# Second block's attention: value products once per head with 512 query columns, and two instead of four buffers for rounded weights in its background

## Chip, cores and metric

The kernel runs on one core of a Trainium2 chip. The metric is the device time of one execution in microseconds (us), the median of the timed runs. Engines: PE is the matmul engine (TensorE), PEld its weight load, DVE is VectorE, ACT is ScalarE, POOL is GpSimd, and SP issues DMAs.

## The reference, cut to what matters

Two transformer-like blocks run one after the other on 512 tokens with 1024 channels, in float32. The change lies in the second block's attention. It has 8 heads of two 64-wide halves and 128-wide values:

```python
def one_block(q_blk):                                   # 128 queries
    s = einsum('bqhcd,bkhcd->bhcqk', q_blk, k) * scale  # c: the two halves
    p = softmax(s, axis=-1)
    p_diff = p[:, :, 0] - lam * p[:, :, 1]
    return einsum('bhqk,bkhd->bqhd', p_diff, v)
```

Around it: `h = rms_norm(x)`; `q, k, v, lru_x, lru_g, gates = split(h @ w_in)`; q and k are normalised and rotated; the attention's result is normalised per head and multiplied by `w_attn_o`; `lru_x` goes through a convolution over time and a gated linear recurrence, `lru_g` through a gelu. Both branches are gated, added and multiplied by `w_out`; a mixture of experts follows.

## The kernel before, in words

Activations lie with channels on the 128 partitions and the 512 tokens along the free dimension. The large projections run in a split form (`product3`, line 1045): the weight is rounded to fp32r (the upper part, made by ACT, helper `weights2_upper`, line 1453, which records line 1428), the rest is the lower part (made by DVE, recorded as line 2053, or by POOL, line 2877), and each 128-channel product is 24 matmuls of 512 columns (line 1057). `JOBS_2` is the written list of these products: 16 for q and k, 8 for v, then `lx` 0 to 7, `lg` 0 to 7 and the rest. Upper parts go into four buffers `up2` (two in the tile `o`, two in `zp`) up to job 31, two others after that. ACT rounds a weight four jobs ahead (two ahead from `lg` on).

Products write to `acc`, a ring of four accumulators in PSUM. `accumulator` (line 774) takes the next one and makes PE wait until the reader of the product four before has finished. Each engine's program is in order; nothing but semaphores joins them.

The attention runs in `STEPS2` = 35 steps over 32 items (8 heads, four tiles of 128 queries each; item s is head s // 4, tile s % 4). In step s PE does: scores of item s (two halves, 512 keys, K = 64, line 1133); in steps 4, 8, 13, 17, 21, 26, 30 and 34 one background product `lx` (`background2_at`); the four transposes of item s - 2 (line 1141); the values of item s - 3 (four fp32 matmuls, 128 query columns, line 1150). An fp32 matmul is two records in the trace. DVE does in step s: the maximum of item s (lines 2450, 2451), then `weigh` of item s - 1 (lines 2439 to 2443), which turns two exponentials into the weighed difference. ACT does: two exponentials of item s (line 1752), then, where there is a background product, its copy into `lru_x` (line 1756) and the rounding of a later weight, then the copy of the transposed weights into one of four buffers `probsT2` (line 1765), and the copy of the values' 128 columns into `q2` (line 1768). `probsT2` lies in the tile `upad` (`padf`). POOL takes the low part of a weight (`lx` 4 to 7) in front of the convolution of `lx` c = 0 to 3, then the convolution itself (lines 2903 to 2908); c = 4 to 7 have the convolution alone.

Before the loop stand the v product (line 1121), ACT's copies of it (line 1736) with two roundings per group of it, DVE's low parts of jobs 20 to 27 (the v weights' last four and `lx` 0 to 3) and DVE's sums for lambda (lines 2424 to 2433). After it PE has the `lg` products, DVE a chain of small operations named decay.

Of the kernel before, what the change touches and what calls it, by code (L numbers as in the profile page):

```python
# [22 lines left out]
P = 128  # L23
# [53 lines left out]
S = SEQ  # L77
# [122 lines left out]
def program(nc, a, out, known=None, debug=None):  # L200
    n = Counts(known)
    mark, at, now = n.mark, n.at, n.now
    with ExitStack() as ctx:
# [124 lines left out]
        padf = upad[:, :, :].rearrange("p c t -> p (c t)")  # L328
        probsT2 = [padf[:, i * S:(i + 1) * S].rearrange("p (j q) -> p j q", j=QT) for i in range(4)]
        cos2, sin2 = trig[:, 0, 0:S], trig[:, 1, 0:S]  # L330
# [222 lines left out]
        job_no2 = {x[0]: i for i, x in enumerate(JOBS_2)}  # L553
        EARLY2 = job_no2["lg", 0]
        up2 = [x[:, :, :].rearrange("p c t -> p (c t)")[:, i * D:(i + 1) * D].rearrange("p (k m) -> p k m", k=DC)
# [4 lines left out]
        def weight2_up(i):  # L560

            return up2[i % 4] if i < EARLY2 else up2_late[i % 2]

# [8 lines left out]

        LOW_BY_POOL = [job_no2["lx", c] for c in range(4, DC)]

# [190 lines left out]
        def _(pe):  # L765
# [378 lines left out]

            def values2(s):
                hd, i = items2[s]
                pe.wait_ge(act_evacuated, at(act_evacuated, ("t2", s)))
                dst = accumulator(("o2", s), act_evacuated)
                for j in range(QT):
                    ins = nc.tensor.matmul(dst[:, 0, 0:P], v2[:, j, hd * P:(hd + 1) * P], probsT2[s % 4][:, j, :],  # L1150
                                           start=(j == 0), stop=(j == QT - 1))
                done(ins, ("o2", s))

            for s in range(STEPS2):
                if s < len(items2):
                    scores2(s)
                for c in background2_at(s):
                    product3(("lx", c), act_evacuated, h2_up, h2_low)
                if 2 <= s < len(items2) + 2:
                    turn2(s - 2)  # L1160
                if s >= 3:
                    values2(s - 3)
            for c in range(DC + LAG):
# [236 lines left out]
        def _(act):  # L1400
# [53 lines left out]
            def weights2_upper(i):  # L1454

                if i < len(JOBS_2):
                    label, name, j = JOBS_2[i]
                    slot = place2[name]
                    act.wait_ge(w2_loaded[slot], at(w2_loaded[slot], name))
                    if i < 4:  # L1460
                        act.wait_ge(psum_filled, at(psum_filled, ("ym" if i < 2 else "out", DC - 1)))
                    elif i == EARLY2:
                        act.wait_ge(dve_made, at(dve_made, ("qkr", 2 * DC - 1)))
                    elif i == EARLY2 + 1:
                        act.wait_ge(psum_filled, at(psum_filled, ("t2", len(items2) - 1)))
                    else:
                        act.wait_ge(psum_filled, at(psum_filled, job_done(i - (4 if i < EARLY2 else 2))))
                    upper(weight2_up(i), columns2(name, j), ("wup",) + label)
# [263 lines left out]
            for g in range(4):  # L1732
# [5 lines left out]
                for j in range(2):  # L1738
                    weights2_upper(2 * DC + 4 + 2 * g + j)

            act.wait_ge(dve_made, at(dve_made, "lam_sums"))
            made(nc.scalar.activation(small[:, 10:12], small[:, 8:10], ACT.Exp), "lam_exp")
            for s in range(STEPS2):
# [11 lines left out]
                for c in background2_at(s):  # L1755
                    evacuated(nc.scalar.activation(lru_x[:, c, 1:1 + S], result2(("lx", c)), ACT.Copy), ("lx", c))
                    if job_no2["lx", c] + 4 < EARLY2:
                        weights2_upper(job_no2["lx", c] + 4)
                if s == STEPS2 - 4:
                    weights2_upper(EARLY2)  # L1760
                if 2 <= s < len(items2) + 2:
                    src = result2(("t2", s - 2)).rearrange("p (j q) -> p j q", j=QT)
                    if s >= 6:
                        act.wait_ge(psum_filled, at(psum_filled, ("o2", s - 6)))
                    evacuated(nc.scalar.activation(probsT2[(s - 2) % 4], src, ACT.Copy), ("t2", s - 2))
                if s >= 3:
                    hd, i = items2[s - 3]
                    evacuated(nc.scalar.activation(q2[:, hd, i * P:(i + 1) * P], result2(("o2", s - 3))[:, 0:P],
                                                   ACT.Copy), ("o2", s - 3))
            weights2_upper(EARLY2 + 1)  # L1770
            act.wait_ge(dve_made, at(dve_made, "neg_abs"))
            made(nc.scalar.activation(decay[:, 1, :], decay[:, 1, :], ACT.Exp), "lam_e")
            def output_squares(c):
                if c >= 2:
                    act.wait_ge(psum_filled, at(psum_filled, ("oss", c - 2)))
                act.wait_ge(act_evacuated, at(act_evacuated, ("o2", len(items2) - 1)))
                made(nc.scalar.activation(tmp[c % 2], q2[:, c, :], ACT.Square), ("sqo", c))
# [218 lines left out]
        def _(dve):  # L1996
# [411 lines left out]
            for c in range(2 * DC + 1):  # L2408
# [8 lines left out]
                if c < 2 * DC:  # L2417
                    weights2_lower(c + 4)
            for i in range(2 * DC + 4, 2 * DC + 12):
                weights2_lower(i)  # L2420
# [101 lines left out]
            for m in range(DC):  # L2522
                if m == 0:
                    dve.wait_ge(act_evacuated, at(act_evacuated, ("o2", len(items2) - 1)))
                if m:
# [244 lines left out]
        def _(pool):  # L2770
# [120 lines left out]
            for c in range(DC):  # L2891
                if c < 4:
                    weights2_lower(job_no2["lx", 4 + c])
                if c == 0:
# [80 lines left out]
```

## Time and profile before

| | us |
|---|---|
| median of 3 runs | 2028.38 (2026.44 to 2030.29) |
| profiled execution | 2031.49 |
| its span | 2029.70 |

| engine | busy us | share of the span |
|---|---|---|
| PE | 1865.5 | 92% |
| PEld | 1550.7 | 76% |
| DVE | 1190.3 | 59% |
| ACT | 891.8 | 44% |
| POOL | 355.7 | 18% |

Busy times are of one execution; the span is the time from its first to its last instruction, the profiled time has 1.79 us around it. The granted clock is PE's, as a share of 2.4 GHz. The attention of the second block runs from 1150.6 to about 1308 us of the span.

### The profile page before, as it was taken

To read this page: it belongs to the slowest core of one execution; us is meant where nothing else is said; L and a number is where in the kernel's file an instruction comes from. 1 tells how busy PE (TensorE), PEld (TensorE's weight loads), DVE (VectorE), ACT (ScalarE), POOL (GpSimd) and SP (SyncE) were. 2 spreads that over 40 slices of the span, in tenths; PEclk is the share of its full clock that TensorE was granted. 3 is DMA by queue.
4 is the path that set the end of the run, shared out by engine and by line. 5 is a ranking of instruction groups with operands and counts; after the bars stand their busy time and mean duration, and the time that the engine had idled before them with its cause. 6 is when DMAs were issued, how large, how long until landed. Compare 5 with 4: busy or idle time off the path is not lost.

```text
span 2029.7 us, 26888 instructions
## 1 busy us (share of the span) xinstructions
PE 1865.5 (92%) x10912; PEld 1550.7 (76%) x10912; DVE 1190.3 (59%) x1628; ACT 891.8 (44%) x1425; POOL 355.7 (18%) x239
## 2 busy tenths in 40 slices
PE   6999999999999999999898888989999997999993
PEld 5988787989997788988676765665568876777772
DVE  5565443445375543543787467567664337788786
ACT  4435433324435443322332355336643235777672
POOL 3332221002333221002311055500000001000001
PEclk9999999999999999999898999999999988999997
DMA  5212102223212202223121200121333237999994
GB/s 170 68 63 68 42 22 83 63 65 123 81 38 88 63 22 84 63 74 128 42 83 42 83 21 22 42 84 42 104 135 107 101 112 275 373 386 379 377 375 166
DMA packets 155949, 241.61 MB, mean 119 GB/s; under 512 B 9313, under 2 KB 100738, under 8 KB 155826
## 3 DMA queue, kind: packets, MB, share of 16 engines
q1 hardware_dynamic: 148450, 213.07, 31.0%
q0 software_dynamic: 4464, 16.25, 2.1%
q10 hardware_dynamic: 2912, 10.55, 1.3%
q8 instruction: 88, 1.44, 0.3%
q14 instruction: 35, 0.29, 0.0%
HBM read 223.61 MB, written 16.25 MB: 118 GB/s over the span
## 4 chain that ended last, share of the span: by engine, by line
PE 77%; DVE 16%; ACT 3%; issue 2%; DMA 1%; POOL 1%; SPq 0%; ACTq 0%; POOLq 0%; DVEq 0%
PE acc L825 27%; PE acc L1057 16%; PE acc L1269 9%; PE acc L1042 4%; PE acc L924 4%; PE acc L988 3%; PE acc L1121 2%; DVE ring_split L2637 2%; PE acc L965 2%; DVE ring_split L2053 1%; DVE v L2388 1%; PE acc L1179 1%; DVE rt L2450 1%; PE acc L842 1%; PE acc L976 1%
## 5 line engine op out<-in xcount | busy, mean ns | idle before, releaser
L825 PE MATMUL acc<-h_split,ring_split 128*128 128x264 f32 x1088 | 310.0, 285 | 0.0
L825 PEld LDWEIGHTS acc<-h_split,ring_split 128*128 128x128 f32 x1088 | 206.2, 190 | 0.0
L1057 PE MATMUL acc<-h_split,ring_split 128*128 128x512 f32 x368 | 146.1, 397 | 0.0
L825 PE MATMUL acc<-h_split,v_split 128*128 128x264 f32 x384 | 111.6, 291 | 19.0 <-DVE ring_split L2053 19.0
L825 PE MATMUL acc<-ring_split,v_split 128*128 128x264 f32 x384 | 109.9, 286 | 0.0
L2388 DVE RECIPROCAL v<-v 128x512 f32<-128x512 f32 x26 | 87.1, 3351 | 27.9 <-ACT v L1706 27.9
L825 PE MATMUL acc<-h_split,krope_split 128*128 128x264 f32 x320 | 94.8, 296 | 4.1 <-ACT latent L1607 2.6
L825 PE MATMUL acc<-ring_split,krope_split 128*128 128x264 f32 x320 | 91.5, 286 | 0.0
L825 PEld LDWEIGHTS acc<-h_split,v_split 128*128 128x128 f32 x384 | 73.4, 191 | 22.0 <-issue 22.0
L2053 DVE TENSOR_TENSOR ring_split<-ring,o_split 128x1024 fp32r<-128x1024 f32 (+1 forms) x32 | 47.0, 1473 | 73.6 <-ACT o_split L1428 73.6
L2921 POOL DMA_INDIRECT latent<-h_rows,rows_of x16 | 18.4, 1148 | 396.8 <-PE acc L1255 229.5
L2791 POOL TENSOR_TENSOR latent<-latent 128x528 f32<-128x528 f32 x18 | 28.5, 1583 | 338.4 <-ACT latent L1423 338.0
L2053 DVE TENSOR_TENSOR ring_split<-ring,v_split 128x1024 fp32r<-128x1024 f32 (+1 forms) x56 | 59.8, 1071 | 44.0 <-ACT v_split L1428 44.0
L1269 PE MATMUL acc<-qk_split,krope_split 128*128 128x512 f32 x240 | 75.8, 397 | 8.5 <-DVE ring_split L2637 6.2
L1057 PEld LDWEIGHTS acc<-h_split,ring_split 128*128 128x128 f32 x368 | 70.2, 191 | 16.3
L2805 POOL TENSOR_TENSOR ring_split<-ring,krope_split 128x1024 fp32r<-128x1024 f32 x20 | 48.3, 2414 | 168.9 <-ACT krope_split L1428 168.9
L988 PE MATMUL acc<-latent,v 128*64 128x128 f32 (+2 forms) x464 | 74.1, 284 | 0.9 <-ACT latent L1627 0.8
L1428 ACT ACTIVATE v_split<-ring 128x1024 fp32r<-128x1024 f32 (+2 forms) x58 | 54.8, 949 | 43.3 <-PE acc L825 41.8
L825 PEld LDWEIGHTS acc<-ring_split,v_split 128*128 128x128 f32 x384 | 73.5, 191 | 0.0
L825 PE MATMUL acc<-work_split,v_split 128*128 128x264 f32 x256 | 72.9, 285 | 0.0
L825 PE MATMUL acc<-upad_split,ring_split 128*128 128x264 f32 x256 | 72.7, 284 | 0.0
L2637 DVE TENSOR_TENSOR ring_split<-ring,qk_split 128x2048 fp32r<-128x2048 f32 x24 | 54.1, 2295 | 27.2 <-ACT qk_split L1924 27.2
(557 smaller groups left out, 5766.8 us busy)
## 6 DMA issues: line engine op xcount, KB each, us to landing
ring<-in_w_in SPq DMA_DIRECT2D x64, 1024.0 KB, 5.3
ring<-in_w_expert_gate SPq DMA_DIRECT2D x13, 2048.0 KB, 10.0
ring<-in_w_expert_up SPq DMA_DIRECT2D x12, 2048.0 KB, 11.1
ring<-in_w_expert_down SPq DMA_DIRECT2D x11, 2048.0 KB, 11.5
ring<-in_w_out SPq DMA_DIRECT2D x12, 1024.0 KB, 5.2
hres<-in_w_expert_down SPq DMA_DIRECT2D x5, 2048.0 KB, 10.9
hres<-in_w_expert_up SPq DMA_DIRECT2D x4, 2048.0 KB, 10.9
y_rows<-gate ACTq DMA_DIRECT2D x16, 512.0 KB, 7.2
```

Of the source, the lines that this page charges most:

```text
L825: ins = nc.tensor.matmul(dst[0:rows_, half, 0:HALF], w[:, k, :], x[:, c], start=(k == 0 and i == 0), stop=(k == last and i == 2), skip_gro ...
L924: ins = nc.tensor.matmul(dst[0:nt, half, 0:width], x, w[:, c], start=(k == 0 and part == 0), stop=(k == count - 1 and part == 2), skip_gro ...
L965: ins = nc.tensor.matmul(dst[0:nt, c0:c1], qT[0:QK, hd, t0:t0 + nt], kT[0:QK, hd, c0:c1], start=True, stop=True)
L988: ins = nc.tensor.matmul(dst[r:r + VD, 0, 0:nt], v[0:nk, j, hd * VD:(hd + 1) * VD], probsT[s % 2][0:nk, j, 0:nt], start=(j == 0), stop=(j ...
L1042: ins = nc.tensor.matmul(dst[:, 0, :], w, rhs(k), start=(k == 0), stop=(k == len(lhs) - 1))
L1057: ins = nc.tensor.matmul(dst[:, 0, :], w[:, k, :], x, start=(k == 0 and i == 0), stop=(k == DC - 1 and i == 2), skip_group_check=True)
L1269: ins = nc.tensor.matmul(dst, x, w, start=start and i == 0, stop=stop and i == 2, skip_group_check=True)
L1428: nc.scalar.activation(dst, src, ACT.Copy).then_inc(act_made, 1)
L2053: made(nc.vector.tensor_tensor(dst, src, up.bitcast(F32), ALU.subtract), label)
L2388: chain(nc.vector.reciprocal(tmp[tile], tmp[tile]))
L2637: nc.vector.tensor_tensor(granule_half(i, half, "low"), granule_half(i, half, "raw"), granule_half(i, half, "up").bitcast(F32), ALU.subtra ...
L2805: nc.gpsimd.tensor_tensor(dst, src, up.bitcast(F32), ALU.subtract).then_inc(pool_made, 1)
```

## The change

1. `values2` is called once per head, behind the transposes of its last tile (steps 6, 10, ... 34): four matmuls with 512 query columns in place of sixteen with 128. ACT copies the result once per head, 512 columns wide.
2. `probsT2` has two buffers for a whole head each, one in `upad`, one in `zp`. ACT waits once per head for a free one.
3. As `zp` is taken, the upper parts of `lx` use the two buffers in `o` alone, and are made two products ahead. `lx` 2 and 3 are no longer rounded before the loop but in it.
4. The low parts of `lx` 2 and 3 go from DVE (before the loop) to POOL (in front of convolutions 0 and 1), so POOL makes six of them.

```diff
-        probsT2 = [padf[:, i * S:(i + 1) * S].rearrange("p (j q) -> p j q", j=QT) for i in range(4)]
+        probsT2 = [x[:, 0:QT * S].rearrange("p (j q) -> p j q", j=QT) for x in (padf, flat_of(zp))]
...
-        EARLY2 = job_no2["lg", 0]
+        EARLY2, LX2 = job_no2["lg", 0], job_no2["lx", 0]
...
-            return up2[i % 4] if i < EARLY2 else up2_late[i % 2]
+            return up2[i % 4] if i < LX2 else up2[i % 2] if i < EARLY2 else up2_late[i % 2]
...
-        LOW_BY_POOL = [job_no2["lx", c] for c in range(4, DC)]
+        LOW_BY_POOL = [job_no2["lx", c] for c in range(2, DC)]
...
-            def values2(s):
-                hd, i = items2[s]
-                pe.wait_ge(act_evacuated, at(act_evacuated, ("t2", s)))
-                dst = accumulator(("o2", s), act_evacuated)
+            def values2(hd):
+                pe.wait_ge(act_evacuated, at(act_evacuated, ("t2", QT * hd + QT - 1)))
+                dst = accumulator(("o2", hd), act_evacuated)
                 for j in range(QT):
-                    ins = nc.tensor.matmul(dst[:, 0, 0:P], v2[:, j, hd * P:(hd + 1) * P], probsT2[s % 4][:, j, :],
+                    ins = nc.tensor.matmul(dst[:, 0, :], v2[:, j, hd * P:(hd + 1) * P], probsT2[hd % 2][:, j, :],
                                            start=(j == 0), stop=(j == QT - 1))
...
-                if s >= 3:
-                    values2(s - 3)
+                if s >= 3 and items2[s - 3][1] == QT - 1:
+                    values2(items2[s - 3][0])
...
-                        act.wait_ge(psum_filled, at(psum_filled, job_done(i - (4 if i < EARLY2 else 2))))
+                        act.wait_ge(psum_filled, at(psum_filled, job_done(i - (4 if i < LX2 + 2 else 2))))
...
                 for j in range(2):
-                    weights2_upper(2 * DC + 4 + 2 * g + j)
+                    if 2 * DC + 4 + 2 * g + j < LX2 + 2:
+                        weights2_upper(2 * DC + 4 + 2 * g + j)
...
-                    if job_no2["lx", c] + 4 < EARLY2:
-                        weights2_upper(job_no2["lx", c] + 4)
+                    if job_no2["lx", c] + 2 < EARLY2:
+                        weights2_upper(job_no2["lx", c] + 2)
...
-                    if s >= 6:
-                        act.wait_ge(psum_filled, at(psum_filled, ("o2", s - 6)))
-                    evacuated(nc.scalar.activation(probsT2[(s - 2) % 4], src, ACT.Copy), ("t2", s - 2))
-                if s >= 3:
-                    hd, i = items2[s - 3]
-                    evacuated(nc.scalar.activation(q2[:, hd, i * P:(i + 1) * P], result2(("o2", s - 3))[:, 0:P],
-                                                   ACT.Copy), ("o2", s - 3))
+                    hd, i = items2[s - 2]
+                    if hd >= 2 and i == 0:
+                        act.wait_ge(psum_filled, at(psum_filled, ("o2", hd - 2)))
+                    evacuated(nc.scalar.activation(probsT2[hd % 2][:, :, i * P:(i + 1) * P], src, ACT.Copy), ("t2", s - 2))
+                if s >= 3 and items2[s - 3][1] == QT - 1:
+                    hd = items2[s - 3][0]
+                    evacuated(nc.scalar.activation(q2[:, hd, :], result2(("o2", hd)), ACT.Copy), ("o2", hd))
...
-            for i in range(2 * DC + 4, 2 * DC + 12):
+            for i in range(2 * DC + 4, LX2 + 2):
                 weights2_lower(i)
...
             for c in range(DC):
-                if c < 4:
-                    weights2_lower(job_no2["lx", 4 + c])
+                if c + 2 < DC:
+                    weights2_lower(job_no2["lx", c + 2])
```

## Rows read from the trace of the kernel before

**Rows 1.** The page's busy times: us, share of the span, instructions.
```profile
PE 1865.5 (92%) x10912; PEld 1550.7 (76%) x10912; DVE 1190.3 (59%) x1628; ACT 891.8 (44%) x1425; POOL 355.7 (18%) x239
```
**Rows 2.** A stretch: its us, busy PE, PEld, DVE, ACT, POOL; granted clock, DMA.
```profile
1210.00:1230.00 20.00, 17.56 (x97) 12.43 (x96) 12.65 (x24) 9.96 (x26) 11.68 (x8) 1.00 0.00 1
```
**Rows 3.** Waits in the loop: who for whom, us in total, times, longest.
```profile
POOL v L2903 <- ACT latent L1756: 32.8, 4, 11.4
...
DVE rt L2450 <- PE acc L1133: 36.8, 8, 5.3
```
**Rows 4.** Chain of waits, one period: start us, length, engine, tile, line.
```profile
1218.92 1.14 DVE rt L2450
...
1222.45 1.15 DVE rt L2450
...
1225.38 5.83 PE acc L1057 x24
...
1233.64 1.24 DVE rt L2450
```
**Rows 5.** PE's timeline there: start us, length, line, form [idle before, what ended it].
```profile
1218.97 0.66 PE L1141 MATMUL acc<-const,krope 128*128 128x128 f32 x4 [1.25 <-DVE krope L2443]
...
1222.51 0.66 PE L1141 MATMUL acc<-const,v 128*128 128x128 f32 x4 [0.93 <-DVE v L2443]
1223.00 1.06 PE L1150 MATMUL acc<-upad,work 128*128 128x128 f32 x8
1223.99 1.13 PE L1133 MATMUL acc<-qk 64*128 64x512 f32 x4
1225.38 0.50 PE L1057 MATMUL acc<-h_split,zp_split 128*128 128x512 f32 x1 [0.26 <-ACT krope L1752]
```
**Rows 6.** PE's timeline later: fp32 products of 512 columns.
```profile
1358.87 1.88 PE L1042 MATMUL acc<-v,ones 128*128 128x512 f32 x4
```
**Rows 7.** Timeline of ACT and DVE at the loop's start.
```profile
1150.68 0.60 ACT L1736 ACTIVATE work<-acc 128x512 f32<-128x512 f32 x1 [5.08 <-PE acc L1121]
...
1151.17 1.99 ACT L1428 ACTIVATE zp_split<-ring 128x1024 fp32r<-128x1024 f32 x2
...
1152.25 2.36 DVE L2053 TENSOR_TENSOR ring_split<-ring,zp_split 128x1024 fp32r<-128x1024 f32 x2 [8.99 <-ACT zp_split L1428]
...
1153.18 1.28 ACT L1742 ACT_TABLE_LOAD   x1
...
1155.42 0.20 ACT L1742 ACTIVATE small<-small 128x2 f32<-128x2 f32 x1 [0.96 <-DVE small L2425]
...
1156.08 1.20 DVE L2450 TENSOR_REDUCE rt<-acc 128x2 f32<-128x1024 f32 x1
```
**Rows 8.** PE's timeline at the loop's end and before lg 2.
```profile
1295.54 1.12 PE L1141 MATMUL acc<-const,gate 128*128 128x128 f32 x4 [2.62 <-DVE gate L2443]
...
1301.54 0.52 PE L1057 MATMUL acc<-ring_split,zp_split 128*128 128x512 f32 x1
...
1321.23 0.47 PE L1057 MATMUL acc<-h_split,trig_split 128*128 128x512 f32 x1 [2.05 <-DVE ring_split L2053]
```
**Rows 9.** PE's timeline behind idle times; by stretch: us, PE busy, granted clock, DMA.
```profile
350.69 0.56 PE L825 MATMUL acc<-h_split,v_split 128*128 128x264 f32 x1 [2.79 <-DVE ring_split L2053]
...
808.49 0.36 PE L825 MATMUL acc<-h_split,v_split 128*128 128x264 f32 x1 [2.79 <-DVE ring_split L2053]
...
1256.13 0.66 PE L1141 MATMUL acc<-const,gate 128*128 128x128 f32 x4 [1.57 <-DVE gate L2443]
...
1321.00:1327.00 6.00, 5.77 (x18) 0.72 0.49 144
...
1509.58 0.51 PE L1057 MATMUL acc<-latent_split,krope_split 128*128 128x512 f32 x1 [1.95 <-DVE o_split L2053]
...
1664.98 6.34 PE L1224 MATMUL acc<-const,h 128*128 128x128 f32 x32
...
1670.00:1671.00 1.00, 1.00 (x9) 0.78 0.01 4
```

More of the change, by code:

```diff
@@ L1143, in turn2 @@
                 done(ins, ("t2", s))
-            def values2(s):
-                hd, i = items2[s]
-                pe.wait_ge(act_evacuated, at(act_evacuated, ("t2", s)))
-                dst = accumulator(("o2", s), act_evacuated)
+            def values2(hd):
+                pe.wait_ge(act_evacuated, at(act_evacuated, ("t2", QT * hd + QT - 1)))
+                dst = accumulator(("o2", hd), act_evacuated)
                 for j in range(QT):
-                    ins = nc.tensor.matmul(dst[:, 0, 0:P], v2[:, j, hd * P:(hd + 1) * P], probsT2[s % 4][:, j, :],
+                    ins = nc.tensor.matmul(dst[:, 0, :], v2[:, j, hd * P:(hd + 1) * P], probsT2[hd % 2][:, j, :],
                                            start=(j == 0), stop=(j == QT - 1))
-                done(ins, ("o2", s))
+                done(ins, ("o2", hd))
             for s in range(STEPS2):
@@ L1775, in output_squares @@
                     act.wait_ge(psum_filled, at(psum_filled, ("oss", c - 2)))
-                act.wait_ge(act_evacuated, at(act_evacuated, ("o2", len(items2) - 1)))
+                act.wait_ge(act_evacuated, at(act_evacuated, ("o2", HEADS - 1)))
                 made(nc.scalar.activation(tmp[c % 2], q2[:, c, :], ACT.Square), ("sqo", c))
@@ L2523, in _ @@
                 if m == 0:
-                    dve.wait_ge(act_evacuated, at(act_evacuated, ("o2", len(items2) - 1)))
+                    dve.wait_ge(act_evacuated, at(act_evacuated, ("o2", HEADS - 1)))
                 if m:
```

## Prediction

> **What bounds the kernel now.** I read the busy times of the page first: the matmul engine works 92% of the span [rows 1], so at most places the kernel goes at its pace. The changed stage is the second block's attention, from 1150.6 to about 1308 us. The busy times of a stretch in its middle show no engine full: PE 17.6, DVE 12.7, ACT 10.0 and POOL 11.7 us of 20, with the clock at 1.00, 2.4 GHz [rows 2]. So waits decide. The table of waits has one large entry on the way: DVE's score maximum waited 36.8 us for the scores, in 8 pieces of up to 5.3 us [rows 3]. The chain of waits over one period says why [rows 4]: steps at DVE's pace (maxima start at 1218.92 and 1222.45, 3.53 apart), then the background product lx (1225.38, 5.83 long), behind it transposes, values and scores, and the next maximum only at 1233.64. From 1222.45 to 1233.64 are 11.2 us for two DVE steps; DVE starves. Seven products lie so inside the loop.
>
> **1. The values.** Before, each of 32 steps has 8 records with 128 columns; they start at 1223.00 and the scores behind them at 1223.99, so they take 0.99 [rows 5]. Per head that is 4 x 0.99 = 3.96. Afterwards a head has 8 records with 512 columns. No fp32 product of this stage has that shape; the ones products of the same engine do, four of them in 1.88 us, each lasting 0.59 [rows 6]: (1.88 - 0.59) / 3 = 0.43 apart, so 8 x 0.43 = 3.44. PE's own work shrinks by about 0.5 us a head, 4 us in all, if all of it were on the path. But it comes as one lump behind every fourth step.
>
> **2. The ring of four accumulators.** Every product takes the next of 4, and waits until the one taken four before is read. Before, in front of lx lie the scores of its step, the values, the transposes and the scores of the step before: lx waits for the exponential of the step before. It shows in [rows 5]: scores start at 1223.99, and lx at 1225.38 after idle time that ACT's exponential ended. Without values in each step that place holds older transposes, read long ago. So nothing but PE's own order holds lx.
>
> **3. One period at full clock.** Transposes start at 1222.51 [rows 5], values would follow at 1223.00. Now scores stand there and hold PE 1.13 less a drain of some 0.07, up to 1224.06; lx then takes its 5.83 less 0.16, as its first matmul doesn't start cold, up to 1229.73; transposes 0.43 (0.66 less the drain), 1230.16; scores to the maximum 1.17, 1231.33, instead of 1233.64. (The three differences are estimates from the starts and durations of rows 4 and 5.) This saves 2.31 where no values come. Products fall in steps 4, 8, 13, 17, 21, 26, 30, 34, and whole heads are multiplied in steps 6, 10, 14, 18, 22, 26, 30, 34, both from the floor rule and from the four tiles a head. So:
> - five products without values in their step: 5 x -2.31 = -11.55;
> - steps 26 and 30 hold both, 3.44 more between product and maximum: 2 x (3.44 - 2.31) = +2.26;
> - steps 6 and 10: transposes 0.49, values 3.44, scores 1.17 make 5.10 us, and 0.06 before it, where DVE needs 3.53 [rows 4]: 2 x 1.63 = +3.26;
> - steps 14, 18, 22 the same, and the values wait for a copy that ACT makes behind the copy of lx and the rounding of a weight; some 0.4 more: 3 x 2.03 = +6.1.
>
> The sum is +0.1: the time won by the earlier product is given back by the lumps. The lower bound lets the five products gain 2.9 each, were DVE and the drains 0.6 quicker there, -3; the upper has the wait of 0.4 in all lumps and 0.5 more at each product, +4.
>
> **4. The start.** ACT rounds two weights (1151.17, 1.99 for both) and DVE takes two low parts (1152.25, 2.36) right behind the v product; then DVE sums lambda, and ACT's exponential is at 1155.42, the first maximum at 1156.08 [rows 7]. These are lx 2 and 3, which move into the loop. DVE's sums then are made during the v product, ACT loads its table (1.28) where the roundings stood, behind the copy that ends at 1151.28, so the exponential falls at 1152.57: -2.85, on the path since scores 0 follow the v product at once. Bounds: 0 (another wait) and -3.5.
>
> **5. The end.** Before, the last product starts at about 1301 (its second matmul at 1301.54), behind transposes and values at half clock: those at 1295.54 last 1.12 [rows 8] instead of 0.66 [rows 5]. Without those two values it starts with the last transposes' end, near 1298.9: -2.1; but it then runs at half clock for some 2 us more, +1.05. Behind it 3.44 instead of 0.99: +2.45; ACT's copy is 512 wide (0.60 instead of 0.28): +0.32. All that follows hangs on this copy: ACT's rounding for lg 1, DVE's low part, the decay work, and PE again at 1321.23 after 2.05 idle [rows 8]. Sum +1.7; bounds 0 and +3.
>
> **6. The background's weights.** Rounding lx 2 to 7 (1.05 each) moves from four products ahead to two. ACT does it behind the copy of each product, POOL takes the low part, now for six products instead of four. A low part and the seven pieces of a convolution are the 8 instructions and 11.68 us of POOL in [rows 2], and a period has 18 us, later perhaps 16; POOL waited 32.8 us in all for lx [rows 3]. The product that reads it comes two periods later. So I count 0; without that cover each product would wait for ACT's rounding (1.0) and POOL's low part, which I put at 2 (DVE takes 1.2, rows 7): 3 each. No DMA is moved: slots of raw weights come free by the same products.
>
> Without the clock the sum is 0.1 - 2.85 + 1.7 = -1.1 us.
>
> **7. The clock.** PE's idle before the transposes in a DVE-paced step is 1.25 and 0.93 [rows 5]; once 1.57, and the clock stayed at 2.4 GHz [rows 9]. Taking 0.99 of values away makes these 2.2, 1.9 and 2.5. The same trace went to 1.2 GHz around idles of 1.95 and 2.05, and 2.62 [rows 8, 9]. There are about 13 such gaps in the new loop, two in each early period, three in the late ones. From 1321 to 1327 the granted clock is 0.72 in the mean [rows 9]: with only the levels 1.0 and 0.5, that is 0.28 x 6 / 0.5 = 3.4 us at half, which loses 1.7 us of PE work if PE is full. In plain steps DVE hides that: transposes and scores doubled (0.86 + 2.12) are 3.0 of 3.5. Before lx or a lump it is paid. I take three falls at 1.2: +3.6. Bounds: none, 0; eight at 1.7, +13.6. That a gap of such length does not always cost is in [rows 9]: of two idles of 2.79 us before the same kind of matmul one was followed by a slow one (0.56), the other by one at its normal 0.36. I take the lower side since half of each fall is hidden in plain steps.
>
> The Trainium skill, "TensorE: Matmul & The Clock Gate", Part 4, holds that transposes don't count as activity for the clock, which would leave the plain steps with scores alone and make most of the 13 gaps fall (about 8, +13.6 instead of +3.6). In this trace 32 transposes run alone from 1664.98 for 6.3 us, and the clock granted from 1670 to 1671, inside them, is 0.78 in the mean [rows 9]: with two levels only, it rose among transposes. So I don't take the rule, though it feeds rival B.
>
> **The sum.** -1.1 + 3.6 = +2.5 us. The profiled execution took 2031.49 (span 2029.70), so it would be 2034.0; the median of the timed runs is 2028.38, 3.1 less, so I say 2030.9. A change within 0.2% (4.06 us) can't be told from none here.
>
> **Rivals.**
> - A: the clock never falls inside the loop. For: gaps of 1.57 passed. Against: 1.95 and 2.05 fell. With sum -1.1 it gives 2027.3; with the low ends of 3 (-3) and 5 (0) it is -5.9, 2022.5. Chance 0.30, about 0.18 of it faster.
> - B (slower): half clock in most gaps, PE's activity being too thin without the values. For: idle grows over the two lengths that fell. Against: gaps are parted by 6 to 9 us of full work. Six to eight falls at 1.7: +9 to +12.5, 2037.5 to 2041. It decides from three falls at 1.7 (-1.1 + 5.1 = +4.0). Chance 0.27.
> - C: lx does not start earlier, as ACT holds an accumulator for another reason. Then only the 0.99 is saved by five products, 5 x 1.32 = 6.6 more: +9, 2037.5. The ring's order speaks against it. Chance 0.05.
> - D: POOL's low parts are late from lx 2 on: 6 x 3 = +18. POOL's slack is against it. 0.03.
>
> The forecast's own case (one to four falls, 2027 to 2033) has 0.35. Faster: 0.18 from A and 0.02 from the forecast's low end, 0.20. Same: 0.12 of A and 0.30 of the forecast, 0.42. Slower: 0.03 of the forecast, B, C and D, 0.38. The range 2023.5 to 2038.5 takes A nearly whole and B's nearer half.
>
> **What would show it.** Step 2: lx starts with no idle after its scores. Step 3: the maximum comes 8.9 us after the one two steps before at lx, instead of 11.2, and 12.3 in steps 26 and 30. Step 4: first maximum 2.8 us nearer to the v product's end. Step 5: 3.4 us from the last lx to its copy. Step 7: granted clock under 1.00 between 1170 and 1290, where it was 1.00. If the clock stays at 1.00 and the loop is still not shorter by 1, my lumps are wrong; if the loop is over 8 us shorter, the price of the lumps is.

## The result, and the profile after

The changed kernel takes 2042.56 us (median of 5 runs, 2042.07 to 2048.88), the kernel before 2029.05 beside it (2026.44 to 2032.23): a ratio of 1.0072, 95% interval 1.0053 to 1.009 (here and below the times are medians; a ratio is worked out from the single executions and can differ a little from the quotient of the medians). It is slower by 13.5 us, and above the range of the prediction. The profiled execution took 2043.05 (span 2041.2) against 2031.49 before. From the first scores of the loop to the decay work behind the last product are 159.9 us before and 173.4 after, so the loss lies in the changed loop. Of the ten executions of the first experiment two were slow (4755.98 and 10062.9 us); they count in its median and not in its ratio.

The busy times of the page, as in [rows 1]:

```profile
PE 1874.4 (92%) x10720; PEld 1535.2 (75%) x10720; DVE 1199.1 (59%) x1626; ACT 889.2 (44%) x1401; POOL 360.1 (18%) x241
```

PE has 192 instructions fewer (32 x 8 values became 8 x 8) and is yet busy 9 us longer. DVE has two instructions fewer and is busy 9 us longer. Work of the same kind has become slower on both.

By stretch (us, busy PE, PEld, DVE, ACT, POOL; granted clock, DMA), the first as in [rows 2]:

```profile
1210.00:1230.00 20.00, 17.03 (x64) 9.06 (x63) 15.44 (x25) 10.08 (x24) 11.99 (x8) 0.91 0.01 1
...
1224.00:1230.00 6.00, 4.03 (x12) 2.07 (x13) 5.80 (x9) 3.07 (x8) 4.46 (x3) 0.72 0.00 0
```

The clock is 0.91 where it was 1.00. The six us of the second row hold 0.28 x 6 / 0.5 = 3.4 us at 1.2 GHz, behind an idle time of PE. From 1170 to 1290 the clock falls six times (near 1177.5, 1198, 1225.5, 1246, 1266.5 and 1287) and is 0.92 in the mean; before it fell there not once and was 1.00. Outside these bounds both kernels have a fall at the loop's start (near 1157 and 1158) and one at its end (1307.5 and 1295). "Falls" below are those from 1170 to 1290.

The waits, as in [rows 3]:

```profile
DVE rt L2450 <- PE acc L1133: 40.3, 13, 6.6
...
POOL v L2903 <- ACT latent L1756: 16.9, 2, 9.7
```

DVE starves as much as before (40.3 us for 36.8), in 13 pieces instead of 8. What the edit was to cure is only cut up differently: a long wait at each product became a shorter one there and another at the values.

The chain of waits over one period, as in [rows 4] (start us, length, engine, tile, line):

```profile
1229.10 5.79 PE acc L1057 x24
1234.89 0.44 PE acc L1141 x4
1235.33 1.06 PE acc L1133 x4
1236.38 0.59 PE acc L1141 x4
...
1237.01 3.70 PE acc L1149 x8
1240.71 1.08 PE acc L1133 x4
...
1241.81 1.24 DVE rt L2450
...
1244.66 1.64 DVE gate L2443
...
1246.35 1.11 PE acc L1141 x4
1247.46 2.01 PE acc L1133 x4
1249.47 0.75 PE acc L1057 x2
```

From product to product are 20.4 us; before, 18.4 (products at 1206.96, 1225.38, 1243.79). The first 12.7 are as forecast: the product, a light step, the values of a head, scores. Then comes one whole step of DVE, 4.5 us from 1241.81 to 1246.35 and not 3.53. And PE, idle during it, comes back at half clock: transposes 1.11 instead of 0.66, scores 2.01 instead of 1.06.

PE's timeline shows the idle time, as in [rows 5] (in brackets the idle before and what ended it):

```profile
1197.51 5.29 PE L1149 MATMUL acc<-zp,work 128*128 128x512 f32 x8
...
1216.63 3.70 PE L1149 MATMUL acc<-upad,work 128*128 128x512 f32 x8
...
1225.97 1.12 PE L1141 MATMUL acc<-const,v 128*128 128x128 f32 x4 [2.94 <-DVE v L2443]
1227.02 2.08 PE L1133 MATMUL acc<-qk 64*128 64x512 f32 x4
```

The idle is 2.94, where before it was 0.93 to 1.57 [rows 5, 9]. The values of a head take 3.70 with a full clock and 5.29 where the clock has just fallen.

And DVE's and POOL's timelines show why a step of DVE takes 4.5:

```profile
1216.05 1.23 DVE L2450 TENSOR_REDUCE rt<-acc 128x2 f32<-128x1024 f32 x1 [3.17 <-PE acc L1133]
1217.31 1.22 DVE L2451 TENSOR_SCALAR rt<-rt 128x2 f32<-128x2 f32 x1
...
1224.29 1.63 DVE L2443 SCALAR_TENSOR_TENSOR v<-v,rt 128x512 f32<-128x512 f32 x1
```
```profile
1216.16 2.34 POOL L2877 TENSOR_TENSOR ring_split<-ring,o_split 128x1024 fp32r<-128x1024 f32 x1 [11.50 <-ACT o_split L1427]
...
1224.06 1.31 POOL L2907 TENSOR_TENSOR v<-v 128x512 f32<-128x512 f32 x1
```

L2451 scales two numbers per partition. It takes 0.17 where it is alone and here 1.22: it ends at 1218.53, when POOL's low part L2877 ends (1218.50). L2443 takes 0.75 alone and 1.63 across POOL's L2907, a piece of the convolution. In the critical step from 1221.43 to 1225.92 the convolution adds 0.25 + 0.30 + 0.88 = 1.43 us to three operations. Over the loop DVE's six operations sum to 115.3 us, before to 104.8. In a run in which POOL has next to nothing to do in the loop (below) they sum to 96.1, so they are stretched by 19.2 us, before by 8.7.

The kernel before has the same operations in another phase:

```profile
1215.22 1.23 DVE L2450 TENSOR_REDUCE rt<-acc 128x2 f32<-128x1024 f32 x1 [5.27 <-PE acc L1133]
1216.48 0.33 DVE L2451 TENSOR_SCALAR rt<-rt 128x2 f32<-128x2 f32 x1
```
```profile
1214.44 2.35 POOL L2877 TENSOR_TENSOR ring_split<-ring,zp_split 128x1024 fp32r<-128x1024 f32 x1 [9.22 <-ACT zp_split L1428]
```

There POOL's low part, which starts when ACT has rounded the weight behind its copy of the product, lay 2.0 us under DVE's wait and under the maximum. Behind the product came values (0.99) ahead of the scores. Without them the maximum comes 1 us earlier against POOL, and L2451 runs into the low part.

The Trainium skill, "SBUF — State Buffer", section "Who interferes with whom", says that DVE and GpSimd share a port pair that is an exclusive lock, that beside a DVE operation in a two-port mode, which a tensor_scalar can enter, the later of the two "fully blocks", and that a tensor_reduce never contends on this chip. The trace agrees in both: L2451, a tensor_scalar, ends with POOL's operation, and all 32 maxima take 1.20 to 1.23 us. Whether L2451 runs in such a mode no run shows.

### The profile page after: what moved, and what is told of

The parts are those of the page before. It is cut to its first block, busy times and chain, and to the rows that moved or that the text cites. A ratio compares the mean times of both kernels' runs of the same rounds, so it can differ in the third digit from the quotient of the medians.

```text
span 2041.2 us, 26434 instructions
## 1 busy us (share of the span) xinstructions
PE 1874.4 (92%) x10720; PEld 1535.2 (75%) x10720; DVE 1199.1 (59%) x1626; ACT 889.2 (44%) x1401; POOL 360.1 (18%) x241
## 4 chain that ended last, share of the span: by engine, by line
PE 79%; DVE 14%; ACT 2%; issue 2%; DMA 1%; POOL 1%; SPq 0%; ACTq 0%; POOLq 0%; DVEq 0%
PE acc L825 27%; PE acc L1057 16%; PE acc L1268 9%; PE acc L1042 4%; PE acc L924 4%; PE acc L988 3%; PE acc L1121 2%; DVE ring_split L2637 2%; PE acc L965 2%; PE acc L1149 2%; DVE v L2388 1%; DVE ring_split L2053 1%; PE acc L1178 1%; PE acc L842 1%; PE acc L1133 1%
## 5 line engine op out<-in xcount | busy, mean ns | idle before, releaser
L2921 POOL DMA_INDIRECT latent<-h_rows,rows_of x16 | 18.1, 1130 | 397.6 <-PE acc L1254 231.2
```

## The experiments

Theory P (POOL): the new phase puts POOL's operations across DVE's critical steps. Theory C (clock): PE's thinner work lets the clock fall. Theory L (lumps): a head's values behind every fourth step make PE and DVE take turns. All runs were timed beside the kernel before. "Stretch" below is the sum of DVE's six operations in the loop less 96.1. "The loop" in us is from its first scores to the decay work, in the profiled execution.

**Values per tile again, with the new buffers of weights.**

```diff
-            def values2(hd):
+            def values2(s):
...
-                if s >= 3 and items2[s - 3][1] == QT - 1:
-                    values2(items2[s - 3][0])
+                if s >= 3:
+                    values2(s - 3)
```

> The changed kernel with the values again per tile (16 products of 128 columns a head, an accumulator for each step), but with its two big buffers, its rounding of lx two products ahead and its six low parts on POOL. Theory (the lump of 512 columns makes the loss): the loop goes at the old pace, clock 1.00 from 1170 to 1290, and the start keeps its gain, so 2026 to 2027 us, 2 to 3 under the kernel before. Rival (the background's weights cost, by POOL's or ACT's order): 2035 or more, and DVE operations in the loop stretched as in the changed kernel.

Measured: 2028.55, ratio 0.9994 [0.9984, 1.0004], 1.5 above the expected range. No fall, stretch 9.1. So the two buffers, the later rounding and two more low parts on POOL cost nothing by themselves; all of the loss comes with the values. The loop is 3.2 us shorter in its profile (156.7), but the median doesn't show it. In this profile the loop starts 2.7 us later than before (1153.31 against 1150.57); over all runs its start varies from 1148.2 to 1153.3, so one profile can't say where the 3.2 go.

**Products of nothing in the gaps,** three of 512 columns, unread, ahead of the wait for the weights of seven steps.

```diff
+                dst = accumulator(("t2", s), act_evacuated)
+                if s + 2 in (6, 10, 16, 20, 24, 28, 32):
+                    for _ in range(3):
+                        nc.tensor.matmul(dst[:, 1, :], ident, v2[:, 0, 0:S], start=True, stop=True)
+                pe.wait_ge(dve_made, at(dve_made, ("p2", s)))
-                dst = accumulator(("t2", s), act_evacuated)
```

> The changed kernel with three fp32 products of 512 columns (2.6 us of PE), whose result nobody reads, ahead of the wait for the weights in steps 6, 10, 16, 20, 24, 28 and 32, where PE idles some 3 us. Theory (half clock): the granted clock stays at 1.00 there and 6 to 7 falls of 1.5 us go: 2032 to 2034. Rival (starving DVE behind the lump and DVE operations stretched by POOL make the loss): 2040 to 2043, clock or not.

Measured: 2039.94, ratio 1.0058 [1.0041, 1.0075], the rival's figure; two falls instead of six, clock 0.96. The idle before the transposes is 0.17 to 0.27 in five of the seven places. But only 2.6 us come back, and stretch goes up from 19.2 to 21.5: with PE sooner back, DVE's steps meet POOL differently. Filling the gaps is no cure, and the clock alone isn't the loss.

**Values of 8 columns instead of 512,** in PE's products and in ACT's copy (leaves out most of the attention's result).

```diff
-                    ins = nc.tensor.matmul(dst[:, 0, :], v2[...], probsT2[hd % 2][:, j, :],
+                    ins = nc.tensor.matmul(dst[:, 0, 0:8], v2[...], probsT2[hd % 2][:, j, 0:8],
```

> The changed kernel with 8 instead of 512 query columns in the values (the attention's result is left out but for 8 columns): no lump, PE even thinner. If the lump is what starves DVE: the loop shrinks by 15 to 25 us, 2018 to 2028, even if the clock falls. If thin work on PE is the cause (my rival B as I put it): the clock falls at least as often and the time stays at 2035 or more.

Measured: 2025.36, ratio 0.9983 [0.9973, 0.9993]. PE has 8 x 2.6 = 21 us less to do, and 17.2 come back. So the lumps are nearly wholly on the path, as the prediction had them. Yet with next to no values at all the kernel is only 3.2 us faster than the kernel before beside it (2028.52); the clock still falls six times and stretch is 14.7. What hurts stays when the values are gone.

**The convolution of POOL on 8 columns** (leaves out most of it), in the changed kernel and in the kernel before.

```diff
-                y, z = tmp[2], tmp[3]
+                y, z = tmp[2][:, 0:8], tmp[3][:, 0:8]
...
-                    x, w = lru_x[:, c, j:j + S], vec2[...]
+                    x, w = lru_x[:, c, j:j + 8], vec2[...]
```

> The changed kernel with POOL's convolution on 8 instead of 512 columns (the rest of it is left out). Theory (DVE's operations are stretched by POOL's): DVE's two-column scaling never lasts over 0.2 us, its weighing never over 0.8; DVE's busy time in the loop falls by 10 us or more, and the time by 5 to 9, 2034 to 2037. If contention is off the path: under 2 us.

> The kernel before with POOL's convolution on 8 instead of 512 columns (the rest is left out). Theory (the change moved DVE's operations under POOL's, and before they fell beside them): DVE's stretch in the loop goes from 10 us to about 1, and the time falls only by 2 to 4, 2025 to 2027, against 18 that the same edit took from the changed kernel. Rival (the convolution costs both the same): 2009 to 2013, and then POOL is no cause of the difference.

Measured: changed 2024.85, ratio 0.9977 [0.9967, 0.9986]; before 2017.82, ratio 0.9943 [0.9925, 0.9961]. The convolution costs the changed kernel 17.7 us and the kernel before 11.2. That is 6.5 of the 13.5. I had expected 5 to 9 and 2 to 4: part of it lies outside the loop, which is shorter by 15.7 (157.7) and 7.3 (152.7). Falls in the changed loop go from six to one with it, so POOL's share in them is large: it makes DVE's steps, and so PE's gaps, longer. Stretch is 5.3, all of it L2451 behind a low part, five times 1.05; in the kernel before it is 0.6.

**POOL's low part behind the convolution.**

```diff
-                if c + 2 < DC:
-                    weights2_lower(job_no2["lx", c + 2])
...
+                if c + 2 < DC:
+                    weights2_lower(job_no2["lx", c + 2])
```

> The changed kernel with POOL's low part of a weight behind the convolution of its turn instead of ahead of it. Theory (where POOL's operations fall against DVE's sets the loss): the five stretches of 1.05 by the low part go or move, all other pieces shift by 3.4 us against DVE; DVE's stretch changes by several us and the time with it, 2035 to 2041, though no work is taken away. Rival (lumps and clock alone): 2042 to 2043.

Measured: 2042.11, ratio 1.0073 [1.0054, 1.0093], stretch 20.8, four falls. This is the rival's figure, not mine: another order of the same operations moves the collisions (stretch 20.8 against 19.2) and wins nothing.

**Values per tile in the unused half of the transposes' accumulator,** so that they take no place in the ring of four; with the old buffers, and with the new ones.

```diff
-                dst = accumulator(("o2", s), act_evacuated)
+                if s + 1 < len(items2):
...
+                    jobs[-1] = (("o2", s), act_evacuated, n.layer)
+                    dst = acc[:, (len(jobs) - 1) % ACCS, 1:2, :]
...
```

> The kernel before, with the values of a tile written into the unused half of the transposes' accumulator of the same step, so that they take no place in the ring of four; 128 columns as before. Theory (the gain of the change is in the ring, where lx no longer waits for the exponential, not in the wide values): lx starts 1.3 us earlier, 7 times, 2019 to 2021, clock 1.00 from 1170 to 1290. Rival (POOL's collisions with DVE eat it, as lx and DVE shift against each other): 2027 or more.

> The same with the change's two large buffers and its rounding two ahead, values per tile: adds the start's 2.8 us, 2016 to 2019. Rival as before: 2026 or more; or the start's gain doesn't reach the end, as in the run with values per tile, then equal to the former.

Measured: 2025.45, ratio 0.9982 [0.9973, 0.9992], and 2024.38, ratio 0.9982 [0.9969, 0.9996]. Both are faster than before, by 3 to 4 us; I had expected 8 to 13. The start's gain of the second doesn't show in its median. The chain of the first shows that the product follows its scores at once (1206.37 + 1.06 = 1207.43):

```profile
1206.37 1.06 PE acc L1133 x4
1207.43 5.75 PE acc L1057 x24
```

The next product is at 1225.51, 18.1 us on, before 18.4. The ring's wait was thus real and worth 0.3 a period, as [rows 5] shows it (0.26 idle); the rest of my 2.31 was the values themselves, which come back as lumps.

**One product of 8 columns per tile, in the kernel before** (leaves out nearly all of the attention's result; ACT copies 8 columns too). This thins PE's work and has neither lumps nor new buffers.

```diff
-                for j in range(QT):
-                    ins = nc.tensor.matmul(dst[:, 0, 0:P], v2[...], probsT2[s % 4][:, j, :],
+                ins = nc.tensor.matmul(dst[:, 0, 0:8], v2[...], probsT2[s % 4][:, 0, 0:8],
```

> The kernel before with one product of 8 query columns instead of four of 128 per tile (the attention's result is left out but for a part); an accumulator per step as before. It takes some 0.7 us from between the transposes and the scores in each step, without lumps and without a change of the ring. Theory (taking this time away moves DVE's scaling under POOL's low part, and thins PE): stretches of up to 1 us appear beside the low parts, DVE's stretch grows from 10 us by 3 or more, PE's idle pieces pass 2 us, and the loop gains less than half of the 0.7 x 7 = 5 it saves behind the products: 2026 to 2029. Rival (no such effect): 2022 to 2024.

Measured: 2031.08, ratio 1.0012 [1.0002, 1.0021]. Taking some 0.7 us of work out of each of 32 steps makes the kernel 2.6 us slower, where I had expected it as fast or 2 us faster. Its loop is 163.4 against 159.9. The granted clock from 1170 to 1290 is 0.83 (PE busy 96.97 us; the columns are those of the stretches above):

```profile
1170.00:1290.00 120.00, 96.97 (x401) 60.63 (x400) 86.00 (x156) 59.37 (x166) 65.17 (x46) 0.83 0.09 27
```

Five falls, and stretch 14.0 instead of 8.7. Both marks of the changed kernel are there without a single lump.

**The same, with the convolution on 8 columns.**

> The kernel before with the thin values (one product of 8 columns per tile) and POOL's convolution on 8 columns; the rest of both is left out. To be set against the kernel before with the short convolution alone (2017.8). If the clock loses time by itself: falls in the loop in PE's gaps of 2 us, and 2018 to 2022 though PE has 0.7 us less per step. If POOL's stretch was the cause of the thin values' loss: no or one fall in the loop, and 2011 to 2014.

Measured: 2018.14, ratio 0.9948 [0.9932, 0.9965], two falls, stretch 3.7. Against 2017.82 with full values the difference is 0.3, for 15 us less work on PE in the stretch from 1170 to 1290 (busy 94.95 against 109.88). By what I had written beforehand this is the outcome in which the clock loses time by itself: two of the five falls stay without POOL's convolution. In the profiles the thin values lengthen the loop by 3.4 with the convolution and shorten it by 2.2 without (150.5 against 152.7). So the larger part of the penalty for thin work comes by way of POOL and a smaller one doesn't, within the noise of some 2 us.

**One us of nothing put back where the values were,** four unread products of 128 columns behind the transposes of the steps with a product of the background.

```diff
+                if len(background2_at(s + 2)) and s + 2 < len(items2):
+                    for _ in range(4):
+                        nc.tensor.matmul(dst[:, 1, 0:P], ident, v2[:, 0, 0:P], start=True, stop=True)
```

> The changed kernel with four fp32 products of 128 columns (1.0 us of PE, read by nobody) behind the transposes of the six steps 4, 8, 13, 17, 21 and 26 (and 30), where they stand between a background product and DVE's next maximum. More work on the path, but DVE's maximum comes 1.0 later against POOL's low part, as before the change. Theory: the five stretches of 1.05 by the low part go and the time does not grow, 2039 to 2043. Rival (no part of the loss is this meeting): the stretches don't matter and the time grows by 6 to 7 us, 2048 to 2050.

Measured: 2042.28, ratio 1.0059 [1.0042, 1.0076]. The phase is put right (the second fence is POOL's):

```profile
1218.05 1.23 DVE L2453 TENSOR_REDUCE rt<-acc 128x2 f32<-128x1024 f32 x1 [4.05 <-PE acc L1133]
1219.31 0.33 DVE L2454 TENSOR_SCALAR rt<-rt 128x2 f32<-128x2 f32 x1
```
```profile
1217.27 2.35 POOL L2880 TENSOR_TENSOR ring_split<-ring,o_split 128x1024 fp32r<-128x1024 f32 x1 [11.49 <-ACT o_split L1430]
```

The scaling is back from 1.22 to 0.33, stretch by the low part is 0.8 instead of 5.3, and all of it is 11.6 instead of 19.2. The time is the changed kernel's, though PE has 7 us more to do. So stretch is no measure of the loss by itself: it counts where it lies on the path. But this also says that the 1.05 at the scaling is mostly not on the path by itself: it lies beside a lump of values, behind which DVE has 0.81 idle (1221.43 in the step above). That the low part costs by holding the convolution back, into the critical step, fits the next run but not the one with the low part behind the convolution, which holds it back no more and took 2042.11; it is not shown.

**Low parts of the background by DVE,** in the steps in which it starves.

```diff
-        LOW_BY_POOL = [job_no2["lx", c] for c in range(2, DC)]
+        LOW_BY_POOL = []
...
+                for c in background2_at(s):
+                    if 2 <= c + 1 < DC:
+                        weights2_lower(job_no2["lx", c + 1])
```

> The changed kernel with the low parts of lx 2 to 7 made by DVE (1.2 us each), behind the weighing in the steps with a background product, where DVE starves, instead of POOL (2.35 each). Theory: the five stretches of 1.05 go, POOL's work is 14 us less and ends earlier, DVE's own 1.2 is partly hidden: 2036 to 2040. Rival (clock and lumps alone): 2042 or more, as DVE has more to do.

Measured: 2038.21, ratio 1.0039 [1.0025, 1.0053], four falls. 4.4 us come back although DVE has six operations more.

**And the convolution on 8 columns besides:** next to nothing of POOL in the loop (leaves out most of the convolution).

> The changed kernel with the low parts by DVE and POOL's convolution on 8 columns (the rest left out): POOL has next to nothing in the loop. Theory: five stretches of 1.05 less than in the changed kernel with the short convolution (2024.9), so 2018 to 2021, and one fall or none in the loop; against 2017.8 (the kernel before with the short convolution) that is the price of the lumps less the gain at the start, 1 to 3. Rival: 2024 or more, the lumps cost 7 by themselves.

Measured: 2019.46, ratio 0.9954 [0.9937, 0.9971], stretch 0 by its definition. No fall until 1287.5, behind an idle time of 2.57 at the loop's end, where the kernel before has one of 2.62 [rows 8]. This is the run on which the case rests most. PE's timeline, two periods:

```profile
1215.16 0.66 PE L1141 MATMUL acc<-const,v 128*128 128x128 f32 x4 [1.51 <-DVE v L2443]
...
1232.70 0.66 PE L1141 MATMUL acc<-const,gate 128*128 128x128 f32 x4 [1.51 <-DVE gate L2443]
```

and DVE's step ahead of the first:

```profile
1212.06 1.23 DVE L2450 TENSOR_REDUCE rt<-acc 128x2 f32<-128x1024 f32 x1 [2.33 <-PE acc L1133]
1213.32 0.17 DVE L2451 TENSOR_SCALAR rt<-rt 128x2 f32<-128x2 f32 x1
...
1214.36 0.75 DVE L2443 SCALAR_TENSOR_TENSOR v<-v,rt 128x512 f32<-128x512 f32 x1
```

DVE's critical step is 3.06 (to 1215.12) instead of 4.49: shorter by the 1.43 read above. PE's gap shrinks by the same, from 2.94 to 1.51; the clock holds; and a period is 17.5 us, not 20.4. The kernel before with the short convolution has 17.4 (transposes at 1199.47, 1216.87, 1234.25).

**The best version:** values per tile in the other half, the new buffers, low parts by DVE.

> Values per tile in the other half of the transposes' accumulator, the change's two large buffers and rounding two ahead, and the low parts of lx by DVE in the 5 us in which it starves: no lump, POOL relieved. Theory: 1 to 3 us under the run with other half and buffers, 2021 to 2024, the best of all. Rival: DVE's work is on the path, 2028 or more.

Measured: 2024.87, ratio 0.997 [0.9956, 0.9985]. It beats both kernels, by 0.2 to 0.3% the one before and by some 0.9% the changed one, and lies 0.9 above the range that I expected. From the version without DVE's low parts it can't be told.

## Why the prediction was wrong

**Steps 1 and 2, the values and the ring: right.** A head's values take 3.45 to 3.70 where the clock is full (3.44 forecast), and the product follows its scores without idle.

**Step 3, one period: right in what PE does, wrong in what DVE does.** Behind a product the next maximum but one comes after 10.6 us (1225.84 to 1236.43), 1.4 of it half clock, so 9.2 for the 8.9 forecast. With a lump it is 5.38 more (to 1241.81), forecast 5.10. But the period leaves one full DVE step on the path, and for it I put 3.53 from [rows 4], a duration that had the collisions of the old phase in it. Here it is 4.5: +1.0 a period. With POOL's convolution short, and in the changed kernel the low parts gone from POOL too, the two run at 17.5 and 17.4 a period, so the "given back by the lumps" of step 3 holds within 0.2.

**Step 4, the start: right.** From ACT's copy of the v product to the first maximum were 5.4 us [rows 7] and are 2.57; the 2.85 forecast came as 2.83. ACT's and then DVE's timeline:

```profile
1151.35 0.60 ACT L1735 ACTIVATE work<-acc 128x512 f32<-128x512 f32 x1 [5.08 <-PE acc L1121]
1151.97 1.28 ACT L1742 ACT_TABLE_LOAD   x1
1153.26 0.20 ACT L1742 ACTIVATE small<-small 128x2 f32<-128x2 f32 x1
```
```profile
1153.92 1.20 DVE L2450 TENSOR_REDUCE rt<-acc 128x2 f32<-128x1024 f32 x1
```

**Step 5, the end: right in kind, and helped by luck.** The timeline of PE and the chain of waits, for [rows 8]:

```profile
1311.23 0.63 PE L1057 MATMUL acc<-ring_split,o_split 128*128 128x512 f32 x1
```
```profile
1311.00 7.20 PE acc L1057 x24
1318.21 3.45 PE acc L1149 x8
...
1333.72 2.33 PE acc L1057 x9
```

From the second matmul of the last product to PE's start on lg 2 are 22.5 us, before 19.7: +2.8. Of this product, lump and copy the forecast had 3.8 (1.05 + 2.45 + 0.32). Up to the decay work it is 4.4 more (13.4 against 9.0), the product's half clock being 1.4; but the decay work is 1.6 shorter (9.1 against 10.7), since fewer of its small operations meet POOL, and that I had not foreseen. Whether the 2.1 ahead of it came can't be read, as the loop in front runs otherwise.

**Step 6, the background's weights on POOL: "So I count 0" is the step that failed.** I asked whether POOL would be late, and it isn't: nothing waits for a low part, and one operation more or fewer is free while the values stay per tile (ratio 0.9994). I didn't ask what POOL's operations do to DVE beside them, though the trace of before had one line of DVE at 0.17 and 0.33, and another at 0.75 and 1.05, with POOL beside the longer ones. A shift of 1 us turned 8.7 us of such stretch into 19.2; with the values per tile the same work on POOL stretches DVE by 9.1. The introduction has it that nothing but semaphores joins the engines. That is wrong: L2451 and L2877 end together with no semaphore between them.

**Step 7, the clock: right in kind, too low in number.** I forecast about 13 gaps of 1.9 to 2.5 and three falls in them. PE catches up with two light steps behind each lump, and then waits for a whole step of DVE, so there is one gap a period, but of 2.9 to 3.0. Six gaps brought six falls here, five of 2.9 to 3.0 and one of 2.6. The length of a gap alone doesn't decide: with values of 8 columns a gap of 1.94 is followed by half clock (the first line, transposes in 1.12), with the low parts by DVE one of 2.90 isn't (the second, in 0.66). A fall costs 1.4 where transposes and scores follow (0.45 + 0.95), and 1.6 where a lump does (5.29 against 3.70). In the changed kernel it isn't a cause by itself: with POOL out of the way the gap is 1.51, and from 1170 to 1287 nothing falls. The measured time lies 1.6 above the upper end of rival B (2037.5 to 2041), and six falls are B's number, but at 1.4 to 1.6 they make only some 9 us. B's cause was PE's thin work; the thin values in the kernel before bear a part of that out, yet here DVE's stretched step opens the gap.

```profile
1218.07 1.12 PE L1141 MATMUL acc<-const,krope 128*128 128x128 f32 x4 [1.94 <-DVE krope L2443]
```
```profile
1175.66 0.66 PE L1141 MATMUL acc<-const,krope 128*128 128x128 f32 x4 [2.90 <-DVE krope L2443]
```

**The sum.** Six periods with 1.0 for DVE's step and 1.4 for the clock are 14.4 us; 3.6 had been taken for the clock, so 10.8 were missing. The profiled execution is 9.05 over the 2034.0 forecast for it. By medians, the difference of 13.5 splits into three (each good to some 2 us); in the loops of the profiles the same three are 3.0, 1.9 and 8.4 of 13.4:

- the changed kernel with POOL emptied, against the kernel before with the short convolution and its four low parts on POOL: 2019.46 - 2017.82 = +1.6, where the sum without the clock was -1.1;
- low parts on POOL, convolution short: 2024.85 - 2019.46 = +5.4. Only 1.9 of it show in the loop of the profiles (157.7 against 155.7); these two profiles differ by 4.0 ahead of the loop, where the kernels are the same, so the rest is not placed;
- the convolution: 17.7 - 11.2 = +6.5.

Theory P is borne out: with POOL's work gone the loss and the clock's falls go together. Theory C holds as its amplifier; in the kernel before with thin values a smaller part of it stands by itself. Theory L alone falls: the lumps are on the path, and cost what the earlier product gains. How much of P's share is DVE's own time and how much the clock's isn't separated beyond the one period read above (1.4 each), since every kernel that changed the clock also changed the phase.

## What to carry to other kernels

Where two engines share a resource, a step's duration belongs to a phase, not to an operation: before moving work, lay the neighbour's timeline beside the critical steps and ask which of them will lie across it afterwards. Taking work off an engine that waits anyway gained nothing here, and lengthened its gaps until its clock fell. Work gathered into a lump behind a starved engine makes the two take turns; here the same values in small pieces, with their wait for an accumulator gone too, took 2024.38 us against 2042.56 in lumps.

## What the runs showed of the hardware

- A DVE operation on two columns takes 0.17 us alone and 1.22 when started 1.15 us into a POOL operation of 2.34: it ends with POOL's (1218.53 and 1218.50).
- POOL is stretched as well: its L2905 takes 1.56 us in one place and 1.88 in another (1222.41 and 1225.46).
- An fp32 product is hardly cheaper below 128 columns. Eight records with 8 columns take 0.96, 0.12 each, where eight with 128 take 1.06 as one row [rows 5]:

```profile
1176.07 0.96 PE L1149 MATMUL acc<-upad,work 128*128 128x8 f32 x8
```

- PE with less to do was slower in clock: with 0.7 us less per step it got 0.83 from 1170 to 1290, where the full work had 1.00.
